# Gate and up of 18 of 22 feed-forward tiles as seven block products in place of eight, in four parts, in a two-layer streaming encoder on one core

## The reference, cut to what matters

```python
def swiglu(x, w_gate, w_up, w_down):
    return (jax.nn.silu(x @ w_gate) * (x @ w_up)) @ w_down

h = h + FFN_RESIDUAL * swiglu(rmsnorm(h, norm_ff1[layer]), ff1_w_gate[layer],
                              ff1_w_up[layer], ff1_w_down[layer])
```

## Time and profile before

| | |
|---|---|
| median of 3 runs | 1954.45 us (1953.42 to 1957.58) |
| the profiled execution, its own time | 1953.96 us |
| its span | 1951.9 us |
| mean granted TensorE clock | 0.994 |
| PE, PEld busy | 1931.4 us (99%), 1814.2 us (93%) |
| DVE, ACT, POOL busy | 967.5 us (50%), 605.0 us (31%), 315.3 us (16%) |
| matmuls | 13943 |
| chain that ended last | PE 93%, DVE 3%, issue 2%, ACT 2% |

### The profile page before, as it was taken

How to read it: one execution, slowest core, us unless ns; L and a number is a source line. 1 busy time by engine, 2 the same in 40 slices (tenths; PEclk the granted TensorE clock), 3 DMA queues, 4 the chain that set the end, 5 groups by cost and what they waited for, 6 DMA issues and landing times.

```text
span 1951.9 us, 33853 instructions
## 1 busy us (share of the span) xinstructions
PE 1931.4 (99%) x13943; PEld 1814.2 (93%) x13943; DVE 967.5 (50%) x1059; ACT 605.0 (31%) x710; POOL 315.3 (16%) x568
## 2 busy tenths in 40 slices
PE   7999999999999999999999999999999999999999
PEld 7999999999999999999999999999877778888887
DVE  5443377566665443344564433445555564433443
ACT  5222222332243222222332222223455332222222
POOL 2888888011130000000000000000011000000000
PEclk9999999999999999999999999999999899999999
DMA  6322544354333323432233323322311133233323
GB/s 176 87 81 82 151 134 151 125 128 129 99 84 87 86 82 88 110 87 70 81 108 88 93 83 102 87 70 81 108 44 44 44 104 90 76 96 108 98 71 90
DMA packets 329026, 185.61 MB, mean 95 GB/s; under 512 B 7288, under 2 KB 322968, under 8 KB 328952
## 3 DMA queue, kind: packets, MB, share of 16 engines
q1 hardware_dynamic: 323280, 166.81, 30.6%
q0 software_dynamic: 5344, 17.69, 3.2%
q10 hardware_dynamic: 328, 0.07, 0.0%
HBM read 173.56 MB, written 9.80 MB: 94 GB/s over the span
## 4 chain that ended last, share of the span: by engine, by line
PE 93%; DVE 3%; issue 2%; ACT 2%; ACTq 0%; POOL 0%; DVEq 0%
PE ps L729 77%; PE ps L948 5%; PE ps L990 2%; PE ps L1009 1%; PE ps L1045 1%; PE ps L1173 1%; PE ps L1141 1%; DVE wl L1464 1%; DVE arena L1845 0%; ACT arena L1410 0%; PE ps L770 0%; PE ps L883 0%; PE ps L909 0%; PE ps L908 0%; PE ps L899 0%
## 5 line engine op out<-in xcount | busy, mean ns | idle before, releaser
L729 PE MATMUL ps<-xl,wh 128*128 128x264 f32 (+1 forms) x2448 | 567.1, 301 | 0.0
L729 PE MATMUL ps<-xh,wh 128*128 128x264 f32 (+1 forms) x2448 | 566.1, 301 | 0.7 <-DVE t_a L1517 0.5
L729 PE MATMUL ps<-xh,wl 128*128 128x264 f32 (+1 forms) x2448 | 565.7, 301 | 0.0
L1464 DVE TENSOR_TENSOR wl<-raw,wh 128x2048 fp32r<-128x2048 f32 x173 | 412.8, 2386 | 168.6 <-ACT wh L1184 168.4
L729 PEld LDWEIGHTS ps<-xh,wh 128*128 128x128 f32 x2448 | 392.3, 188 | 18.0 <-DVE t_a L1517 1.1
L1184 ACT ACTIVATE wh<-raw 128x2048 fp32r<-128x2048 f32 x173 | 329.6, 1905 | 246.7 <-PE ps L729 211.2
L729 PEld LDWEIGHTS ps<-xl,wh 128*128 128x128 f32 x2448 | 391.2, 188 | 15.5 <-issue 0.2
L729 PEld LDWEIGHTS ps<-xh,wl 128*128 128x128 f32 x2448 | 391.1, 188 | 15.1
L729 PE MATMUL ps<-act_l,wh 128*128 128x264 f32 (+1 forms) x1232 | 284.7, 301 | 0.0
L729 PE MATMUL ps<-act_h,wh 128*128 128x264 f32 (+1 forms) x1232 | 284.6, 301 | 0.0
L729 PE MATMUL ps<-act_h,wl 128*128 128x264 f32 (+1 forms) x1232 | 284.3, 301 | 0.0
(11 more groups left out here) (296 smaller groups left out, 1686.8 us busy)
## 6 DMA issues: line engine op xcount, KB each, us to landing
raw<-in_ff_w_gate SPq DMA_DIRECT2D x88, 512.0 KB, 4.0
raw<-in_ff_w_up SPq DMA_DIRECT2D x88, 512.0 KB, 5.2
raw<-in_ff_w_down SPq DMA_DIRECT2D x64, 384.0 KB, 4.0
raw<-in_ff_w_down SPq DMA_DIRECT2D x64, 320.0 KB, 3.7
raw<-in_even_w_in SPq DMA_DIRECT2D x16, 512.0 KB, 5.2
raw<-in_attn_w_qkv SPq DMA_DIRECT2D x12, 512.0 KB, 4.6
raw<-in_even_w_out SPq DMA_DIRECT2D x8, 512.0 KB, 4.7
raw<-in_attn_w_o SPq DMA_DIRECT2D x8, 512.0 KB, 4.5
```

What stands on the lines that cost most here:

```text
L729: last = nc.tensor.matmul(ps[:, 2 * pair + hf, 0:nh], w[:, slot, b * P:(b + 1) * P], x[:, k0 + k, c0 + hf * nh:c0 + (hf + 1) * nh], start= ...
L1464: v.tensor_tensor(wl[:, c % 2, :], raw[:, c % 2, :], wh[:, c % 2, :].bitcast(F32), ALU.subtract).then_inc(wl_ready, 1)
```

## The change

It touches feed-forwards 1, 2 and 3. Each has four parts now: 4 tiles as before, and then three parts of 6 (`PARTS`); after each come 8 down tiles over that part's tiles, with weight units of 4 or 6 blocks. The other 18 tiles are computed in another way.

One such unit treats gate and up of a tile as a 2 by 2 block matrix. Its rows are gate and up, and its columns are the two halves of the 8 feature blocks: A11 and A12 are gate's blocks, A21 and A22 are up's. The input is a 2 by 2 matrix too: the feature halves by the two halves of the columns (264 or 256). In place of eight block products there are seven, of sums of these blocks (Strassen's form with Winograd's order of sums). Each product is 4 blocks by 3 matmuls on half the columns. PE makes them in this order, each into a PSUM bank of its own: A22, S1, A11, A12, S2, S4, S3.

- POOL makes the sums of weights for each unit: S1 = A21 + A22, S2 = S1 - A11, S4 = A12 - S2, S3 = A11 - A21, each 128x512, into `w_sum`. The sums of inputs are made once for each feed-forward (`seven_tables`, first loop, from `xs`, the scaled input that DVE writes).
- ACT and DVE make the high and low parts of the seven forms in five pieces: A22, S1, A11 with A12, S2 with S4, S3. Each form has one place in `wh` and `wl` (`FORM`), so the form of the next unit is written there once the product of this unit has been made.
- ACT copies the second and third product out of PSUM. DVE puts the seven products together with seven adds of half the columns each, five of which read PSUM. The semaphore `used` counts six stages of that for each unit, `prod` counts products, `s_hi`, `s_lo` count pieces of forms. In the code the products are numbered from 0 (`product(0, ...)`), and `prod` reaches 7 * sn + 1 after the first.
- The eight banks are used in rotation: product 2 of a unit takes the bank of product 1 of the unit before, whose read counts as `used` = 6 (`read_out`, code number 0), when both halves of `t_c` are written.
- The input of the seven products is scaled beforehand, so these tiles are not multiplied by `r`. During the first four tiles and the 8 down tiles after them ACT, DVE and POOL make the tables of the input (`table_high`, `table_low`, `half_high`, `half_low`).
- Attention's constants on POOL wait for the seven-product units of feed-forward 2, since both use the same scratch space.

The diff, cut to its core:

```diff
+    RF = 4
+    PARTS = [RF] + [(NF - RF) // 3] * 3
+    SU = NF - RF
...
+        HB = XH * P
+        FORM = {"S2": 0, "S4": HB, "S3": 2 * HB, "S1": 4 * HB, "A22": 5 * HB, "A11": 6 * HB, "A12": 7 * HB}
...
+                for _, _, sn, _, c in seven_units(n):
+                    a11, a12, a21, a22 = (raw[:, c % 2, x * HB:(x + 1) * HB] for x in range(4))
+                    s1, s2, s4, s3 = (w_sum[:, x * HB:(x + 1) * HB] for x in range(4))
+                    pool.wait_ge(raw_landed[c % 2], 32 * (c // 2 + 1))
+                    if sn:
+                        pool.wait_ge(s_lo, 4 * (sn - 1) + 2)
+                    g.tensor_tensor(s1, a21, a22, ALU.add).then_inc(sform, 1)
+                    pool.wait_ge(sform, 4 * sn + 1)
+                    if sn:
+                        pool.wait_ge(s_lo, 4 * (sn - 1) + 4)
+                    g.tensor_tensor(s2, s1, a11, ALU.subtract).then_inc(sform, 1)
+                    pool.wait_ge(sform, 4 * sn + 2)
+                    g.tensor_tensor(s4, a12, s2, ALU.subtract).then_inc(sform, 1)
+                    pool.wait_ge(wl_ready, c)
+                    g.tensor_tensor(s3, a11, a21, ALU.subtract).then_inc(sform, 1)
+
+            seven_tables(1, ALL)
+            seven_tables(2, ALL)
+            pool.wait_ge(used, 6 * 2 * SU)
+            pool.wait_ge(wl_ready, ATT[0] - KD)
...
-                for nf in PART:
+                for nf in PARTS if n else PART:
...
+            def read_out(sn, x):
+                return (copied, 2 * sn + x) if x in (1, 2) else (used, 6 * sn + (6, 0, 0, 1, 2, 3, 5)[x])
...
+                def product(x, form, x_h, x_l):
+                    if free[x]:
+                        pe.wait_ge(*free[x])
+                    for k in range(XH):
+                        at = slice(FORM[form] + k * P, FORM[form] + (k + 1) * P)
+                        nc.tensor.matmul(ps[:, banks_[x], 0:nh], wh_flat[:, at], x_h[k], start=(k == 0), stop=False)
+                        nc.tensor.matmul(ps[:, banks_[x], 0:nh], wh_flat[:, at], x_l[k], start=False, stop=False)
+                        last = nc.tensor.matmul(ps[:, banks_[x], 0:nh], wl_flat[:, at], x_h[k], start=False, stop=(k == XH - 1))
+                    last.then_inc(prod, 1)
...
+                product(0, "A22", table(tf_h, 2), table(tf_l, 2))
+                pe.wait_ge(s_lo, 4 * sn + 2)
+                product(1, "S1", table(tf_h, 0), table(tf_l, 0))
+                pe.wait_ge(s_lo, 4 * sn + 3)
...
+                pe.wait_ge(s_lo, 4 * sn + 4)
+                product(4, "S2", table(tf_h, 1), table(tf_l, 1))
...
+                pe.wait_ge(wl_ready, c + 1)
...
+                            pe.wait_ge(wl_ready, u + s + 2 * i + 1)
+                            pe.wait_ge(tile_evac, j + s + 2 * i - 1)
+                            pe.wait_ge(act_ready[n], done - 1)
+                            if own:
+                                pe.wait_ge(used, 6 * own[-1][2] + (6 if s else 2))
+                            mm3((s + flip) % 2, (u + s) % 2, range(nf), act_h, act_l, 0, col,
+                                lambda: pe.wait_ge(act_ready[n], done)).then_inc(tile_full, 1)
...
+                        if pending is not None:
+                            act_high(*pending)
+                        if nxt:
+                            forms_a(nxt[2], nxt[4], (prod, 7 * sn + 1), (prod, 7 * sn + 2))
+                        if sn >= 2:
+                            act.wait_ge(used, 6 * (sn - 1))
+                        for x in (1, 2):
+                            act.wait_ge(prod, 7 * sn + x + 1)
+                            nc.scalar.activation(o_sum[:, sn % 2, x - 1, 0:nh], ps[:, banks_[x], 0:nh], ACT.Copy).then_inc(copied, 1)
+                        if nxt:
+                            forms_b(nxt[2], nxt[4], (prod, 7 * sn + 4))
+                            forms_c(nxt[2], nxt[4], (prod, 7 * sn + 6))
+                        else:
+                            act.wait_ge(prod, 7 * sn + 2)
+                            split_high(c + 1, 0, 0, nf * P)
+                        act.wait_ge(used, 6 * sn + 4)
+                        silu(k)
+                        if nxt:
+                            forms_d(nxt[2], nxt[4], (prod, 7 * sn + 7))
+                        pending = (k, f)
...
+            def form_low(sn, names, src, c=None):
+
+                at = slice(FORM[names[0]], FORM[names[0]] + len(names) * HB)
+                v.tensor_tensor(wl_flat[:, at], src, wh_flat[:, at].bitcast(F32), ALU.subtract).then_inc(wl_ready if names[0] == "S3" else s_lo, 1)
...
+                        if nxt:
+                            forms_a(nxt[2], nxt[4])
+                        else:
+                            split_low(c + 1, 0, nf * P)
+                        dve.wait_ge(prod, 7 * sn + 4)
+                        dve.wait_ge(copied, 2 * sn + 2)
+                        v.tensor_tensor(t_a[:, first], p1, bank(3), ALU.add).then_inc(used, 1)
+                        if nxt:
+                            forms_b(nxt[2], nxt[4])
+                        dve.wait_ge(prod, 7 * sn + 5)
+                        v.tensor_tensor(u2, p1, bank(4), ALU.add).then_inc(used, 1)
+                        dve.wait_ge(prod, 7 * sn + 6)
+                        v.tensor_tensor(w_, p5, bank(5), ALU.add).then_inc(used, 1)
+                        dve.wait_ge(used, 6 * sn + 3)
+                        v.tensor_tensor(t_a[:, second], u2, w_, ALU.add).then_inc(used, 1)
+                        if nxt:
+                            forms_c(nxt[2], nxt[4])
+                        dve.wait_ge(prod, 7 * sn + 7)
+                        v.tensor_tensor(u3, u2, bank(6), ALU.add).then_inc(used, 1)
+                        dve.wait_ge(used, 6 * sn + 5)
+                        dve.wait_ge(act_ready[n], k)
+                        v.tensor_tensor(t_c[:, first], u3, bank(0), ALU.add)
+                        v.tensor_tensor(t_c[:, second], u3, p5, ALU.add).then_inc(used, 1)
+                        dve.wait_ge(used, 6 * sn + 6)
+                        dve.wait_ge(silu_done[n], k + 1)
+                        gate(k)
+                        if nxt:
+                            forms_d(nxt[2], nxt[4])
+                        act_low(k, f)
...
+                    for d in range(KD):
+                        if d + 1 < KD:
+                            split_low(u + d + 1, 0, nf * P)
+                        elif nxt:
+                            forms_a(nxt[0][2], nxt[0][4])
+                            forms_b(nxt[0][2], nxt[0][4])
+                        elif n < 3:
+                            split_low(u + KD, 0)
+                        if part == 0 and d < 4:
+                            half_low(d)
+                        residual(d, j + d, (d + (part in (1, 2))) % 2, 0.5, more, col)
+                    if nxt:
+                        forms_c(nxt[0][2], nxt[0][4])
+                        forms_d(nxt[0][2], nxt[0][4])
```

More of the change, by code:

```diff
@@ L808, in down @@
                                 output_tile(2 * i + s - 1)
-                    if n == 3 and part == 1:
+                    if n == 3 and part == 3:
                         for i in range(KD // 2):
@@ L1231, in ffn, with down @@
                     done += nf
-                    def down(i, last=False):
+                    def down(i):
                         for s in range(2):
[L1235 to L1239, removed]
-                                norm_input(m + 1, s + 2 * i, col, (tile_evac, j0 + s + 2 * i + 1))
@@ L1242, in ffn @@
[L1242 to L1248, removed]
+                            split_high(u0 + s + 1, i, j0 + s + 2 * i)
+                            if part == 1:
+                                norm_input(m + 1, s + 2 * i, col, (tile_evac, j0 + s + 2 * i + 1))
@@ L1249, in ffn, with form_high, forms_a @@
+                    with act.Fori(0, KD // 2) as i:
+                        down(i)
                     u0 += KD
                     j0 += KD
+            def form_high(sn, c, names, src, free):
+                at = FORM[names[0]]
+                act.wait_ge(*free)
+                nc.scalar.activation(wh_flat[:, at:at + len(names) * HB], src, ACT.Copy).then_inc(wh_ready if names[0] == "S3" else s_hi, 1)
+            def forms_a(sn, c, free_1, free_2):
+                act.wait_ge(raw_landed[c % 2], 32 * (c // 2 + 1))
+                form_high(sn, c, ["A22"], raw[:, c % 2, 3 * HB:4 * HB], free_1)
+                act.wait_ge(sform, 4 * sn + 1)
+                form_high(sn, c, ["S1"], w_sum[:, 0:HB], free_2)
@@ L1459, in _, with split_low @@
             v = nc.vector
[L1461 removed]
+            def split_low(c, i, width=UNITW):
                 dve.wait_ge(wh_ready, c + 2 * i + 1)
[L1464 removed]
+                v.tensor_tensor(wl[:, c % 2, 0:width], raw[:, c % 2, 0:width], wh[:, c % 2, 0:width].bitcast(F32), ALU.subtract).then_inc(wl_ready, 1)
             def tile(pair, col):
@@ L1534, in ffn, with down @@
                     done += nf
```

(16 more changed lines are left out.)

276 lines of the change are left out of this document (257 added, 19 removed).

## The result

The changed kernel takes 2048.3 us, median of three executions from 2042.1 to 2054.5, and the kernel before 1956.0 in the same comparison: the ratio is 1.047, 95% interval 1.043 to 1.052. The forecast was 1969, its range ended at 1996. The direction was right, the size was not: the range missed by 52 us. The profiled execution took 2042.08 us with a span of 2040.3, 88.4 more than the span before; the forecast added 14.5.

The account below looks back on a forecast made before the run. The prediction took PE, busy 99% of the span, to bound the kernel. Its terms, -1.9 - 1.9 + 4.5 for the units and +13.8 for ends of parts, gave +14.5 us: 1969 us, range 1940 to 1996.

Parts of the forecast that it names:

- PE's saving: Seven-product units: 10.28 us of PE in feed-forwards 1 and 2, 9.98 in 3; PE alone would save 73.5 us.
- the line through two paces: Feed-forward 3: matmul pace at 256 columns, 118.8 ns, drawn from the paces at 264 and 512 columns.
- The loop between units, POOL left out: ACT and DVE steps before a unit's second product stop PE 1.11 us, making 11.39 us a unit.
- POOL's part: POOL's weight sums take turns with DVE's SBUF reads: S2 adds 0.17 us, S1 0.35, loop 11.91.
- Each part of 6 has one unit at PE's pace and five of the loop: Units in sum: 1.9 us less in each of feed-forwards 1 and 2, 4.5 more in feed-forward 3.
- Ends of parts: Stops where gate and up units and down tiles change over: 4.6 us a feed-forward, 13.8 in all.
- costed at nothing: Residual adds, smaller splits, input tables, load issue and POOL's attention constants lie beside other work and add no time.
- The clock falls: Rival: PE's stops drop the clock, 6.7 us a fall, one in each part makes 60: 2029 us, chance 0.05.
- The full DVE rival: DVE's own load with POOL's adds held in full bounds the unit at 12.5 us: 1996 us, chance 0.18.

Follow-up runs that it names:

- experiment 1: Changed kernel with GpSimd's four weight sums of each unit made on 16 columns in place of 512: 1952.2 us, ratio 0.997 to the kernel before.
- experiment 5: Changed kernel with each of GpSimd's four weight sums replaced by three constant fills that read nothing: 1962.9 us, ratio 1.003 to the kernel before.
- experiment 4: Kernel before, still eight products, with feed-forwards 1 to 3 in parts of 4, 6, 6 and 6 tiles: 1982.4 us, ratio 1.012.
- experiment 2: Changed kernel with VectorE's low part of S2 and S4 moved behind both t_c adds: 2002.1 us, ratio 1.021 to the kernel before.

## Why the prediction missed

**PE's saving: right.** A unit without other holds takes 11.24 us less the stop of 0.94 that its starts show (the wait of 0.78 and the slower restart), 10.30 against 10.28. In feed-forward 3 the first experiment's units took 11.0 with a stop of 1.04: 9.96 against the 9.98 taken from the line through two paces.

**The loop between units, POOL left out: right.** 11.39 was forecast, 11.24 measured (experiments 1 and 5).

**POOL's part: the mechanism was right, both terms too small.** The stop is 0.78 us without GpSimd's reads, 1.34 where S2 holds t_c second, and 2.16 where S1 holds t_a second too. So S2 adds 0.56, not 0.17, and S1 0.82, not 0.35: 11.24 + 1.38 = 12.62. The price was read from a row whose operation takes 1.07 us; these take 1.3 even where they start first, and start at the worst moment: S1 began 0.01 us ahead of t_a second, where 0.39 was forecast, and held it in full.

**"Each part of 6 has one unit at PE's pace and five of the loop": the step that failed most among the units.** Its first stop comes out of another state. The forecast followed one unit in its steady round and never the change from down units to it, when low parts of three units and GpSimd's sums are all ready and alternate. Nine such stops took 39.7 us in start to start times where nine loops would have stopped PE for 14.8. The 36 others took 62.7, forecast 59.3; that they come so close is luck, since the middle ones are longer than forecast and the last of each part, which has no next unit to prepare, is shorter. In all 102.4 against 74.1: 28 of the 74 missing us, 25 of them at the heads of parts.

**Ends of parts and "costed at nothing": too small.** The other stops of the feed-forwards are 24.0 us, of which the kernel before has 1.0: 23.0 against 13.8, 9 of the missing us (the 23 us of experiment 4 are largely made up of other stops). Feed-forward 1 has 2.7 at the third tile, 2.0 at its exit, and 0.9, 0.7, 0.7 and 0.7 between. The tables of the input were named as free beside 11.7 us tiles. Timeline of VectorE there:

```profile
635.82 2.29 DVE L1729 TENSOR_TENSOR wl<-raw,wh 128x2048 fp32r<-128x2048 f32 x1 [1.10 <-ACT wh L1344]
638.03 2.80 DVE L1861 SCALAR_TENSOR_TENSOR arena<-h,vec,r 128x528 f32<-128x528 f32 x4
640.75 1.86 DVE L1866 TENSOR_TENSOR act_l<-arena,act_h 128x792 fp32r<-128x792 f32 x2
642.54 0.70 DVE L1884 TENSOR_TENSOR t_a<-ps,r 128x528 f32<-128x528 f32 x1
```

They have room in a tile, but they stand ahead of the gate tile's eviction, for which PE stands from 640.8 on. The work had cover by its amount and none by its place. The exit stop is the next stage's full split of 2048 columns behind a down tile of 4.4 us where there were 7.3 before. VectorE and then TensorE at the end of feed-forward 1:

```profile
1013.90 2.29 DVE L1729 TENSOR_TENSOR wl<-raw,wh 128x2048 fp32r<-128x2048 f32 x1 [1.03 <-ACT wh L1344]
...
1016.25 0.51 PE L798 MATMUL ps<-xh,wh 128*128 128x264 f32 x2 [1.86 <-DVE wl L1729]
```

**"The clock falls": the largest term that the sum left out, 31 us, with the wrong size and the wrong chance.** I took one fall of 16 us, from attention, at 6.7 us; the feed-forwards show 17 falls at 1.8 us each, nearly twice the nine for about a quarter of the price. I kept it as a course of its own with a chance of 0.05, and the forecast had nothing for it. Twelve of the 17 follow the nine heads of parts and the three stops in a third tile, which the forecast did not have; the other five follow stops of 2.0 to 2.4 in the steady units. The other executions had a mean clock of 0.971 and 0.967 and took 2048.3 and 2054.5 us, against 0.976 and 2042.1: the spread of this kernel goes with the clock. That stops make it fall is read from their order in time, and from experiment 1, where stops of 0.94 us every 11.24 us left it at full speed; no run changed the clock alone.

**The budget.** -73.5 (PE) + 102.4 (unit stops) + 23.0 (other stops) + 31 (clock) = 83, with 2.2 of attention and -0.6 ahead of the feed-forwards 84.6, against 88.4 measured. The 4 us left are in short stops and in the counting, and stay unassigned. Against the forecast +14.5 the sum lacked 31 of clock, 25 at the heads of parts, 9 of other stops, 3 in the other unit stops and 2 in attention.

**The full DVE rival** (12.5 a unit, 1996) had the period nearly right and the end wrong by 52 us, for the same two reasons: heads of parts and clock. A sum of both engines' turns fits the unit of experiment 2. The prediction's chances took its rivals as exclusive; here the turns and the falls of the clock came together.

## What to carry to other kernels

Fewer matmuls pay only if the elementwise work that replaces them has a free engine, and GpSimd is none for VectorE if both read SBUF: count the turns (here 6.8 + 5.2 us against PE's 10.3) before the chain. Moving the sums to VectorE and the low part off the chain turned 4.7% slower into 1.6% faster than the kernel before.

Work out the first round after each change of phase by itself, since queues are full there, and check a piece of work called hidden by what stands behind it in its queue, not only by its amount. Several engines near their limit make a long stop likely, and in the changed kernel every stop of over 2.6 us was followed by some us of TensorE at half speed: price the clock in the sum and not as a case apart.

## What was not expected of the hardware

- GpSimd's add of 512 columns from two plain operands takes 1.27 to 1.37 us in the median of S2, S3 and S4 (1.26 at least); the 1.07 of the earlier trace rows is, by the code, a product with a broadcast operand.
- Where both queues held such work (the head of a part, 689 to 694 us), the engines took turns, one instruction each, and a VectorE step waits for a whole one of GpSimd's: 0.68 became 1.80 us.
- Single stops of TensorE inside otherwise full stretches were followed by 3.4 to 6.1 us of work at the 1.2 GHz level: in the changed kernel's feed-forwards after each of the twelve of over 2.6 us and after five of some twenty from 1.9 to 2.5; stops of 1 us never. In experiment 1 a stop of 2.7 us at 643.1 had no such fall and one of the same length at 1027.1 had, so length alone does not decide. The Trainium skill describes such a fall and recovery at each gap of a loop (TensorE: Matmul & The Clock Gate, section "HAM oscillation — how this bites in real kernels"); the trace agrees in kind, with 0.76, 0.50 and 0.88 in the three windows across a stop.
